# How a decoder step's expert biases reach TensorE: all at once with a one-hot pick, or one row by DMA for each expert

## What is computed

```python
logits = x @ router_w + router_b
top_logit, top_e = lax.top_k(logits, 4)            # of 32 experts
gate = softmax(top_logit)
# for each block of rows that belong to expert e:
    h = xblk @ w_gu[e] + b_gu[e]                   # 1024 -> 2048, b_gu[e] has 2048 values
    hg, hu = jnp.split(h, 2, axis=-1)
    hg = jnp.minimum(hg, 7.0); hu = jnp.clip(hu, -7.0, 7.0)
    act = (hu + 1.0) * hg * sigmoid(1.702 * hg)
    y = act @ w_down[e] + b_down[e]                # 1024 -> 1024
# y times its gate is added to its token's row
```

## Time and profile before

| | us |
|---|---|
| median of three runs | 1529.06 |
| the profiled execution, whole | 1529.06 |
| its span, first to last instruction | 1527.1 |
| PE busy in the span | 1442.9 (94%) |
| DVE busy | 529.1 (35%) |
| ScalarE (ACT) busy | 287.6 (19%) |
| GpSimd (POOL) busy | 107.2 (7%) |
| chain that ended last: PE / DMA / SP's queue | 64% / 13% / 11% |

### The profile page before, as it was taken

One profiled execution on the slowest core, in us unless ns is written; L12 is line 12 of the kernel. 1 busy time (PEld: TensorE's weight loads), 2 busy tenths in 40 slices (PEclk: granted clock), 3 DMA queues, 4 the chain that ended last, 5 costly groups with the idle time before them and its releaser, 6 DMA issues.

```text
span 1527.1 us, 24420 instructions
## 1 busy us (share of the span) xinstructions
PE 1442.9 (94%) x9323; PEld 684.6 (45%) x9323; DVE 529.1 (35%) x1138; ACT 287.6 (19%) x501; POOL 107.2 (7%) x174
## 2 busy tenths in 40 slices
PE   6977899999999989999999999999999999999995
PEld 4755568866665543333333333333333333333332
DVE  6878665533312142322222222232232213122223
ACT  3111332211313321111111111111111111111111
POOL 1189600000000000000000000000000000000000
PEclk9998899997999989999999999999999999999997
DMA  7853111012668639999999999999999999999992
GB/s 310 179 119 62 56 62 58 31 57 77 271 234 331 245 125 420 415 418 419 418 416 419 419 416 417 418 419 416 418 419 419 415 419 418 417 416 419 418 417 110
DMA packets 86661, 471.60 MB, mean 309 GB/s; under 512 B 7952, under 2 KB 13200, under 8 KB 46928
## 3 DMA queue, kind: packets, MB, share of 16 engines
q1 hardware_dynamic: 80320, 460.89, 74.6%
q10 hardware_dynamic: 6288, 9.95, 3.5%
HBM read 465.07 MB, written 5.74 MB: 308 GB/s over the span
## 4 chain that ended last, share of the span: by engine, by line
PE 64%; DMA 13%; SPq 11%; DVE 5%; issue 4%; ACT 2%; DVEq 0%; ACTq 0%
PE bank L999 16%; DMA big<-in_w_gu 13%; SPq L520 10%; PE bank L1029 10%; PE bank L576 10%; PE bank L949 5%; PE bank L1048 3%; PE bank L659 2%; PE bank L829 2%; PE bank L753 1%; PE bank L963 1%; PE bank L955 1%; ACT big L1283 1%; PE bank L1008 1%; PE bank L745 1%
## 5 line engine op out<-in xcount | busy, mean ns | idle before, releaser
L999 PE MATMUL bank<-big 128*64 128x512 f32 x2048 | 454.1, 596 | 8.3 <-DMA big<-in_w_gu 7.7
L999 PEld LDWEIGHTS bank<-big 128*64 128x64 f32 x2048 | 141.9, 137 | 306.9 <-issue 268.7
L1029 PE MATMUL bank<-big 128*64 128x512 f32 x1024 | 226.8, 595 | 0.0
L1842 DVE TENSOR_TENSOR big<-big,bank 128x320 f32<-128x320 f32 x256 | 104.6, 479 | 344.4 <-PE bank L1048 344.4
L576 PE MATMUL bank<-big 128*128 128x320 f32 (+1 forms) x688 | 186.8, 430 | 2.2 <-ACT big L1228 1.3
L576 PEld LDWEIGHTS bank<-big 128*128 128x128 f32 x688 | 131.1, 192 | 56.5 <-issue 4.9
L1827 DVE TENSOR_SCALAR big<-bank 128x512 f32<-128x512 f32 x32 | 22.2, 693 | 321.8 <-PE bank L999 321.8
L1029 PEld LDWEIGHTS bank<-big 128*64 128x64 f32 x1024 | 71.0, 137 | 133.1 <-issue 127.7
L1297 ACT ACTIVATE big<-big 128x512 f32<-128x512 f32 x32 | 20.2, 632 | 515.5 <-DVE big L1827 515.5
L1081 ACT ACTIVATE big<-bank 128x320 f32<-128x320 f32 (+3 forms) x122 | 53.1, 435 | 248.4 <-PE bank L576 57.2
L949 PE MATMUL bank<-big 128*64 128x512 f32 x396 | 94.1, 610 | 0.2 <-issue 0.2
(11 more groups left out here) (359 smaller groups left out, 1222.8 us busy)
## 6 DMA issues: line engine op xcount, KB each, us to landing
big<-in_w_gu SPq DMA_DIRECT2D x256, 1024.0 KB, 19.6
big<-in_w_down SPq DMA_DIRECT2D x128, 1024.0 KB, 22.4
big<-in_dense SPq DMA_DIRECT2D x47, 1024.0 KB, 8.1
big<-u_windows ACTq DMA_DIRECT2D x32, 160.0 KB, 7.6
out_y<-big SPq DMA_DIRECT2D x3, 512.0 KB, 2.6
big<-in_smw SPq DMA_DIRECT2D x1, 1408.0 KB, 19.5
big<-in_xT SPq DMA_DIRECT2D x2, 640.0 KB, 4.6
big<-in_consts SPq DMA_DIRECT2D x1, 1028.5 KB, 14.6
```

What stands on the lines that cost most here:

```text
L999: last = mm(ps[bank][part, :], xte[:, k, :], w[:, at:at + 512], start=False, stop=(k == KT - 1))
L1029: last = mm(ps[4][part, :], actT[:, k % 4, (k // 4) * CAP:(k // 4 + 1) * CAP], w[:, k % 2, s * 512:s * 512 + 512], start=(k == 0), stop=(k ...
L1842: tt(part, part, ps[bank][:, 0:T], add).then_inc(psum_free[bank], 1)
```

## The change

The tile `pick`, its setup and DVE's copy for each expert go. `bias` holds one expert at a time: its first half on partition 0, its second half on partition 32, and zeros on all the others, written once by a memset of the whole tile (semaphore `bias_zero`). `biasrow` is ones on partitions 0 and 32, set once. SP loads expert 0's two rows, waits until `start_bias` has read them (new semaphore `bias_used`, which the last bias matmul raises), and loads expert 1's; and in `load_expert`, behind chunk 11, it waits for `bias_used` again and loads the next expert's two rows of 4 KB. PE waits for their arrival (`bias_in`) instead of for `bias_picked`. The matmuls keep their shapes.

```diff
@@ SP @@
+            sp.wait_ge(S("bias_zero"), 1)
             for half in range(2):
-                sp.dma_start(BIG[NE * half:NE * half + NE, BIAS:BIAS + FF], a["b_gu"][0:NE, half * FF:half * FF + FF]).then_inc(S("bias_in"), 16)
+                sp.dma_start(BIG[32 * half:32 * half + 1, BIAS:BIAS + FF], a["b_gu"][0:1, half * FF:half * FF + FF]).then_inc(S("bias_in"), 16)
+
+            def load_bias(it, e):
+
+                sp.wait_ge(S("bias_used"), it + 1)
+                for half in range(2):
+                    sp.dma_start(BIG[32 * half:32 * half + 1, BIAS:BIAS + FF],
+                                 a["b_gu"][bass.ds(e + 1, 1), half * FF:half * FF + FF]).then_inc(S("bias_in"), 16)
+
+            load_bias(0, 0)
 
             def load_expert(it, e):
...
                     sp.dma_start(expert_dst(j), expert_chunk(j, e)).then_inc(ring_full[EXPERT_SLOT[j]], 16)
+                load_bias(it, e)
@@ PE @@
-                        mm(ps[bank][part, :], biasrow[row, :], bias[row, s * 512:s * 512 + 512], start=True, stop=False)
+                        last = mm(ps[bank][part, :], biasrow[row, :], bias[row, s * 512:s * 512 + 512], start=True, stop=False)
+                last.then_inc(S("bias_used"), 1)
...
             pe.wait_ge(S("bias_in"), 32)
-            pe.wait_ge(S("bias_picked"), 1)
             start_bias()
...
-                pe.wait_ge(S("bias_picked"), it + 2)
+                pe.wait_ge(S("bias_in"), it * 32 + 64)
                 start_bias()
@@ DVE @@
                 if n == 2:
+                    step(v.memset(bias, 0.0), "bias_zero")
                     step(v.memset(view(ROWS, 72), 0.0))
                     for r in range(4):
                         step(v.memset(quarters[32 * r:32 * r + 1, :], 1.0))
-                    step(tt(pick[:, 0:NE], con("ident")[0:2 * NE, 0:NE], con("ident")[0:2 * NE, NE:2 * NE], add))
-                    step(cp(pick[:, NE:], pick[:, 0:1]))
-                    step(cp(biasrow[0:2 * NE, :], over(pick[:, 0], 1, CAP)), "bias_picked")
+                    for r in range(2):
+                        step(v.memset(biasrow[32 * r:32 * r + 1, :], 1.0))
...
                 dve.wait_ge(S("activated"), it + 1)
-                cp(biasrow[0:2 * NE, :], pick[:, bass.ds(e + 1, 1)].to_broadcast([2 * NE, CAP])).then_inc(S("bias_picked"), 1)
```

More of the change, by code:

```diff
@@ L150 @@
 _w = Regions(PROB)
-(BIAS, XTE, HG, HU, SIG, HACT, ACTT, YB, SELG, SEL, GTT, TAB, CUR, GFIN, RB, SCR, BDOWN, GATET, ROWS, PICK) = (
-    _w.take(n) for n in (FF, KT * CAP, 512, 512, 512, 512, 512, 512, TT * P, TT * CAP, T, 6 * (NE + 1), 8, D, NE, 1200, 2 * P, T, 72, NE + 1))
+(BIAS, XTE, HG, HU, SIG, HACT, ACTT, YB, SELG, SEL, GTT, TAB, CUR, GFIN, RB, SCR, BDOWN, GATET, ROWS) = (
+    _w.take(n) for n in (FF, KT * CAP, 512, 512, 512, 512, 512, 512, TT * P, TT * CAP, T, 6 * (NE + 1), 8, D, NE, 1200, 2 * P, T, 72))
 assert _w.at <= RX
@@ L454, in build @@
         gfin, rbias, bdown, gateT = view(GFIN, D), view(RB, NE), view(BDOWN, 2, P), view(GATET, T)
-        pick = view(PICK, NE + 1, hi=2 * NE)
         biasrow, quarters, ysum = view(ROWS, CAP), view(ROWS + CAP, 1), view(GATET, T)
```

## The result

The changed kernel takes 1538.96 us (median of 5 runs, 1538.61 to 1541.33) against 1529.06: a ratio of 1.0062 with the interval [1.0049, 1.0076]. The forecast was 1539.1 us, slower. Size and sign came out; of the mechanism, half.

What follows compares the result with a forecast made beforehand. The weight stream, 30.13 us an expert against PE's 29.09, was taken to bound the kernel. Row loads of 30 x 2 x 0.175 = 10.5 us, less 0.5, all else 0, gave 1529.06 + 10.0 = 1539.1 us, range 1533.8 to 1541.5.

Steps and rivals of the forecast that it cites:

- What bounds the kernel: Expert loop: weight stream needs 30.13 us an expert, PE 29.09; after some 16 experts the stream paces everything.
- DVE's copy, the 128 KB load, the memset, PE's wait, SP's wait and issues, all at 0: Setup and loop: removed and added work falls into idle time or slack; each taken 0, setup's range 0 to 0.5 us.
- The stream: Pairs of 4 KB rows among the expert weights: 60 small DMAs at 0.175 us, less 0.5, net +10.0 us.
- the 14 ns for the semaphore packet: Each small DMA: a packet's fixed part, added to the 164 ns data packet; bounds 0 to a whole 164 ns.
- the 0.5 us of forgiveness: End of the weight stream: deducted in case the loaded engine runs ahead of the others; range 0 to 1.25 us.
- One engine carries both rows: Each pair in the loop: both one-row DMAs go to the same engine, giving 1539.1 us; chance 74%.
- Rival 2: Each pair's two DMAs fall on different engines: at most 5.3 us each, 1534.3 us, slower by 0.35%; chance 7%.
- a small DMA costs one engine and the other fifteen nothing: Weight stream: a one-packet run is carried by one engine, costing it 178 ns, 175 with the overlap.
- Rival 1: Each row spread over all 16 engines, 256 B each: 2.2 us in all, 1531.3 us; chance 10%.
- Rivals 3, 4 and 5: 1548 us, dearer small DMAs; 1523, copy removal gains; pair late at bias matmuls. First and third 7%, second 2%.
- the rate and the share were to fall to 413 and 1.01: Second half's weight stream: from 418 to about 413 GB/s, DMA share from 1.02, as fifteen engines wait for one.
- The checks on the issues (66), on the 4096 B packets: Signs in the profile: 66 b_gu issues, 4096 B packets growing by 66 less 64, expert period 30.48 us.

Runs made afterwards that it cites:

- e4: Changed kernel without the row loads of experts 1 to 31 and without SP's wait for bias_used; ratio 1.0000 against the kernel before.
- e3: Changed kernel with the two one-row DMAs issued from ACT's queue, SP having neither wait nor issues; 1539.03 us, kernel before 1531.81 on that chip.
- e2: Changed kernel with one DMA of two rows, on partitions 0 and 32, in place of two one-row DMAs; ratio 1.0062.
- e8: Against the kernel with one two-row DMA on partitions 0 and 32, second row moved to partition 64; ratio 1.0038.
- e9: Changed kernel with the second row on partition 64 instead of 32, still two one-row DMAs; ratio 1.0064.
- e10: Changed kernel with the rows on partitions 64 and 96, two one-row DMAs; landing +0.42 us an expert instead of +0.32, total time not given.
- e1: Changed kernel with each row read and written as 16 gapped pieces of 256 B, spread over the engines; 1544.26 us.
- e5: Changed kernel with each row loaded a second time, to partitions 64 and 96, where nothing reads it; +0.69 us an expert against 0.31.
- e7: Changed kernel with each row read onto 16 partitions (0 to 15, 32 to 47), biasrow's ones made sixteenths; 1586.56 us, ratio 1.0356.
- e6: Kernel before the change with w_down read in runs of 8192 B instead of 4096 B, transposes taking every second column; 1521.69 us, ratio 0.9940.

## Why the prediction was right, step by step

- **What bounds the kernel: right.** The weight stream paced before and after; PE kept its 29.09 us an expert, and 0.31 us an expert in the stream, 30 times (9.4), came out as 9.58 us at the end, though PE was on the chain in the first half. The backlog ran out at 946 us (said: near 945).
- **DVE's copy, the 128 KB load, the memset, PE's wait, SP's wait and issues, all at 0: right.** e4 measured 1.0000 with all of them but the loads and SP's part; e3 took SP out with no gain. No bias matmul waited for its rows, so the slack of 1.7 us was never used up.
- **The stream, 60 x 0.175 less 0.5 = +10.0: right in the sum, made of two errors.** Measured are 9.58/60 = 0.160 us a row on the chain, 0.157 in the landings. That is the 164 ns of the data packet over the overlap (164/1.018 = 161); the 14 ns for the semaphore packet were not there, and neither was the 0.5 us of forgiveness. Each was inside the bounds given for it. The two errors nearly cancel: 60 x 0.014/1.018 = 0.8 us too much for the semaphore packets, 0.5 too little for the forgiveness. The trace gives a semaphore packet 0.010 us, but the landings don't grow by it.
- **"One engine carries both rows": right, but only half of the cause.** One engine is late, by 10.2 us. Rival 2 (two engines, 1534.3) would have been wrong even where its condition holds: e2 puts the rows on two engines and costs the same, since both go into one port. The step that failed is "a small DMA costs one engine and the other fifteen nothing"; in e8 three engines are late (by 5.7, 5.5 and 4.8 us) for two rows, and in e9 a second one (by 4.3) though one carries both: an engine pays that carries nothing extra, in stretched packets. The number came out because in the changed kernel the carrying engine is also the one behind that port. That was luck: nothing in the working looked at partitions, and the same working would have given the same number for e10 (measured +0.42 an expert instead of +0.31).
- **Rival 1 (spread over 16 engines, 2.2 us, 1531.3): its condition didn't hold**, the packets under 512 B grew by 34 (7952 to 7986), not by hundreds. And its price was wrong: e1 has the condition, and cost 0.9% instead of 0.14%. The Trainium skill's note on one-row tiles (DMA: Bandwidth & Descriptors, rules for kernel authors), by which a split row fans out, speaks of engines only and leaves open which form is faster; under a full stream e1 found the split dearer.
- **Rivals 3, 4 and 5** had nothing: 0.16 us a row instead of 0.32; no gain from the copy; no wait at the bias matmuls.
- **A check that failed: the rate and the share were to fall to 413 and 1.01.** They stayed at 418 and 1.02. I had the fifteen other engines wait for the sixteenth. They don't: they run ahead, here by up to 10.2 us, so the average in the middle hides the late one, and all of the loss stands in the last 10 us of the stream, as one engine at work and fifteen done. The checks on the issues (66), on the 4096 B packets (46928 to 46964, which are 34 small ones and 2) and on the period (30.48; 30.43 measured) held.

What stays open: why two rows into a port that another engine feeds cost 0.1 to 0.17 us an expert too much (e10, e5), what holds the leading engines at some 10 us, and how the cost of reading one row onto 16 partitions divides. Between the pair on one engine with one port and a placement with different engines and ports, nothing cheaper was found than e8's 0.17 us an expert; a load of all biases ahead of the loop, as the kernel before has it, costs nothing that shows (e4: 1.0000 without it).

## What to carry to other kernels

When a weight stream fills all DMA engines, a small load inside it costs its whole packet, over and over, on the engine that carries it and, where another engine feeds the port it goes into, on that one too, and the sum is to be made per engine and per port, not over the mean of sixteen. Load such rows once, ahead of the stream, even where that takes more bytes and a copy on an idle engine. A DMA share that hasn't moved clears nobody: look at the last microseconds of the stream and at how far a chunk's 16 shares land apart.

## What the runs showed of the hardware

- The destination partition of a 4 KB row changes its price: on 32 beside 0 the pair costs 0.30 us an expert, on 64 beside 0 it costs 0.17 (e2, e8), with the same DMA otherwise.
- A row that comes into a port from another engine stretches weight packets: one or two an expert, by 0.14 to 0.16 us together, with 8192 B packets of up to 0.48 us instead of 0.33 (e8, e9); where the row's engine feeds the port itself, none is stretched (changed kernel; experts 3 to 13).
- An engine and a port are equally full as far as can be told. A row of 4096 B in 0.157 us is 26.1 GB/s; an engine's sixteenth of a 1 MB chunk in 2.485 us is 26.4. The Trainium skill (SBUF — State Buffer, the same section) gives 435 GB/s for the 16 ports, by which one would have 27.2, an estimate close above both.
- DMA engines of one queue don't keep step. In the changed kernel they drift apart by 10.2 us by the last expert, with the leaders still at their old period; in e5, e10 and e1 the lead stops growing at 10.1 to 10.9 us, and the leaders slow down. In e7 it grew to about 14.
- A semaphore packet behind a single data packet had no cost that could be told from 0 (0.157 us a row, against 0.161 for the data packet alone). Packets of 4096 B cost 3% more a byte than those of 8192 B (2.56 against 2.485 us a chunk). That was worth 0.6% of the whole kernel (e6).
- A row cut into 16 pieces for 16 engines was a third dearer than the whole row on one (0.42 against 0.31), since they meet at one port.
